# Sample key steps moved out of the prompt's attention into the projections, with GpSimd taking three of four of the first 80 key products

## What is computed

```python
def _project(x, pos, norm1_w, w_in, q_norm_w, k_norm_w):
    h = _rmsnorm(x, norm1_w)
    p = h @ w_in
    ...
    q = _rope(_rmsnorm(q, q_norm_w), pos)
    k = _rope(_rmsnorm(k, k_norm_w), pos)
    return q, k, v, u

def _scores(q, k):
    s = jnp.einsum('bqhcd,bkhcd->bhcqk', q, k, preferred_element_type=jnp.float32)
    return s * (QK_DIM ** -0.5)

def _diff_attn_sample(q, k_new, v_new, k_past, v_past, lam):
    s = jnp.concatenate([_scores(q, k_past), jnp.where(causal, _scores(q, k_new), NEG)], axis=-1)
    a = _diff_weights(s, lam)
    o_past = jnp.einsum('bhqk,bkhd->bqhd', a[..., :n_past], v_past.astype(jnp.float32))
    ...
```

## Time and profile before

| | us |
|---|---|
| median of 3 runs | 1733.65 (1730.45 to 1736.07) |
| the profiled execution | 1735.41 |
| its span in the trace | 1733.7 |
| TensorE busy | 1474.0 (85%) |
| VectorE busy | 782.4 (45%) |
| ScalarE busy | 356.0 (21%) |
| GpSimd busy | 96.7 (6%) |
| DMA, mean over the span | 345 GB/s, 598.10 MB |

### The profile page before, as it was taken

The page is one execution under the profiler, slowest core; times in us unless marked ns, Lnnn a source line. Parts: engine busy times, 40 slices in busy tenths (PEclk is TensorE's granted clock), DMA queues, the critical chain, the costliest instruction groups (busy, mean ns, idle before and its releaser), DMA issues.

```text
span 1733.7 us, 32093 instructions
## 1 busy us (share of the span) xinstructions
PE 1474.0 (85%) x11950; PEld 595.0 (34%) x11951; DVE 782.4 (45%) x1160; ACT 356.0 (21%) x822; POOL 96.7 (6%) x173
## 2 busy tenths in 40 slices
PE   3868887779788978899998998999899999899970
PEld 2433333346433354332332332333233332232320
DVE  2789879997786335221332232132132131131326
ACT  3212212222222111111211211212112122121220
POOL 0000010000000000000100000000000000000000
PEclk8989995679898857999999999999899999999995
DMA  9557888988998785598999999999999999999986
GB/s 327 182 187 258 283 295 272 331 279 292 311 301 270 242 352 207 227 392 339 429 420 403 427 417 396 412 418 411 392 421 412 401 428 411 397 428 399 428 351 253
DMA packets 127292, 598.10 MB, mean 345 GB/s; under 512 B 20503, under 2 KB 20517, under 8 KB 102026
## 3 DMA queue, kind: packets, MB, share of 16 engines
q1 hardware_dynamic: 109088, 560.20, 81.9%
q10 hardware_dynamic: 8634, 20.00, 3.4%
q0 software_dynamic: 9504, 17.06, 2.6%
HBM read 589.36 MB, written 25.87 MB: 355 GB/s over the span
## 4 chain that ended last, share of the span: by engine, by line
PE 40%; DMA 19%; DVE 2%; issue 1%; ACT 0%; DVEq 0%; SPq 0%; ACTq 0%
PE bank L1511 25%; DMA wts<-in_w_gate_up 16%; PE bank L1548 8%; PE bank L1530 4%; DMA wts<-in_w_down 3%; PE bank L1501 1%; PE bank L1618 1%; DVE v_ring L2139 1%; PE bank L1559 1%; PE bank L1599 0%; DVE q_b L2139 0%; DMA h_tok<-h_rows,v_tok 0%; ACT k_T L1155 0%; DVEq L2127 0%; ACT k_T L1138 0%
## 5 line engine op out<-in xcount | busy, mean ns | idle before, releaser
L1511 PE MATMUL bank<-wts,h_T 128*32 128x512 f32 x4032 | 443.9, 597 | 9.7 <-DMA wts<-in_w_gate_up 5.2
L2061 DVE TENSOR_SCALAR q_T<-bank 128x512 f32<-128x512 f32 x32 | 22.1, 692 | 636.9 <-PE bank L1511 636.9
L1511 PEld LDWEIGHTS bank<-wts,h_T 128*32 128x32 f32 x4032 | 129.5, 111 | 308.3 <-issue 296.4
L1548 PE MATMUL bank<-wts,k_T 128*32 128x512 f32 x2048 | 228.3, 597 | 8.0 <-issue 4.9
L1530 PE MATMUL bank<-wts,h_T 128*32 128x512 f32 x992 | 132.6, 675 | 52.2 <-DMA wts<-in_w_gate_up 50.4
L1658 DVE TENSOR_TENSOR wts<-wts,q_b 128x1024 f32<-128x1024 f32 x128 | 158.1, 1235 | 23.1 <-DMA wts<-in_cache_k 17.4
L1661 DVE TENSOR_REDUCE sc<-wts 128x16 f32<-128x1024 f32 x128 | 156.2, 1220 | 4.4
L1145 ACT ACTIVATE h_T<-bank 128x512 f32<-128x512 f32 x66 | 35.9, 595 | 573.5 <-PE bank L1501 573.5
L1548 PEld LDWEIGHTS bank<-wts,k_T 128*32 128x32 f32 x2048 | 64.9, 110 | 149.0 <-issue 139.5
L1223 PE MATMUL bank<-wts,h_T 128*8 128x128 f32 (+1 forms) x480 | 92.7, 465 | 12.3 <-ACT h_T L854 6.4
L1155 ACT ACTIVATE k_T<-bank 32x256 f32<-32x256 f32 x256 | 95.7, 374 | 13.6 <-PE bank L1548 10.2
(11 more groups left out here) (330 smaller groups left out, 1375.8 us busy)
## 6 DMA issues: line engine op xcount, KB each, us to landing
wts<-in_w_gate_up SPq DMA_DIRECT2D x126, 2048.0 KB, 15.8
wts<-in_w_down SPq DMA_DIRECT2D x64, 2048.0 KB, 18.3
wts<-in_cache_k SPq DMA_DIRECT2D x256, 256.0 KB, 3.7
v_ring<-in_cache_v SPq DMA_DIRECT2D x160, 256.0 KB, 3.8
wts<-in_cache_v SPq DMA_DIRECT2D x96, 256.0 KB, 3.9
wts<-in_w_in SPq DMA_DIRECT2D x5, 2048.0 KB, 24.1
wts<-y_rows SPq DMA_DIRECT2D x4, 2048.0 KB, 15.1
wts<-in_w_out ACTq DMA_DIRECT2D x8, 512.0 KB, 6.2
```

Source lines behind the costliest of these rows:

```text
L1511: m = nc.tensor.matmul(PS[part][p0:p0 + 32, :], lhs[:, 32 * b:32 * b + 32], rhs[:, part * F + half * 512:part * F + half * 512 + 512], sta ...
L1548: m = nc.tensor.matmul(PS[4][p0:p0 + 32, :], act_T[0][:, k, a0:a0 + 32], chunk[c][:, k, n * 512:(n + 1) * 512], start=(c == 0 and k == 0), ...
```

## The change

Three things are changed together.

1. The weights in `SCHEDULE`. In the projections of tiles 2 to 4 each stage now brings 1.45 key steps where it brought 1. In the attention each unit brings 0.2 where it brought 1.4 in two places, and the norm's place 0 where it brought 1. The values' weights stay as they are. The number of key steps in the table's other parts stays too.
2. Of the first 80 groups, those whose number modulo 4 is 0, 1 or 2 have their product on GpSimd, as two pieces of 128x512 (`PIECE = 512`) that signal `kprod_done`. VectorE waits for these counts and does the reduction alone. Group 3 of each four, and all from 80 on, stay with VectorE as before. GpSimd now walks through the same table; its tap products come at units 4 to 7 of the attention in that table, behind all of its key products, and its index tables in part L.
3. The semaphores `xw_loaded` and `y_loaded` become one, `rows_in`.

```diff
+        KEYS = 1.45
         for s in range(1, TILES + 1):
             if s > 1:
-                plan(("P", s), 1, both=s > 2)
-            plan(("P", s - 1), 1 if s > 1 else 0, both=s > 2)
-            plan(("P", s), 1 if s > 1 else 3, both=s > 2)
+                plan(("P", s), KEYS, values=1 if s > 2 else 0)
+            plan(("P", s - 1), KEYS if s > 1 else 0, values=1 if s > 2 else 0)
...
-            plan(("P", s), 1)
-            plan(("P", s), 1, 1, 1, both=True)
+            plan(("P", s), KEYS)
+            plan(("P", s), *[KEYS] * 3, values=1)
             if s < TILES:
-                plan(("P", s + 1), 1, both=True)
-            plan(("P", s), 2, values=1)
-            plan(("P", s), 1, 1, both=True)
+                plan(("P", s + 1), KEYS, values=1)
+            plan(("P", s), 2 * KEYS, values=1)
+            plan(("P", s), *[KEYS] * 2, values=1)
             if s < TILES:
-                plan(("P", s + 1), 1, both=True)
-        plan(("P", TILES), 1, 1, both=True)
+                plan(("P", s + 1), KEYS, values=1)
...
-                plan(("Q", j), 1, both=True)
+                plan(("Q", j), 0.2, values=1)
...
-                plan(("Q", j), 0.4, values=0.7)
+                plan(("Q", j), 0, values=0.7)
...
-                plan(("N", (j - 1) // H), 1, both=True)
+                plan(("N", (j - 1) // H), 0, values=1)
...
+        PIECE = 512
+        KEYS_ON_POOL, KEYS_SHARED = (3, 4), 80
+
+        def on_pool(n):
+
+            return n < KEYS_SHARED and n % KEYS_ON_POOL[1] < KEYS_ON_POOL[0]
+
+        def first_on_pool(b):
+
+            return next((g for g in range(NG) if on_pool(b * NG + g)), None)
+
+        def products_on_pool(n):
+
+            return sum(on_pool(m) for m in range(n + 1)) * GP * (AW // PIECE)
...
+            def key_step(b, g):
+                r, n = g % RING, b * NG + g
+                if not on_pool(n):
+                    return
+                if first_on_pool(b) == g:
+                    pool.wait_ge(qb_in, 32 if b == 0 else 16 * (b + 1))
+                pool.wait_ge(k_full[r], 16 * GP * (4 * b + g // RING + 1))
+                for p in range(GP):
+                    for c0 in range(0, AW, PIECE):
+                        cols = slice(c0, c0 + PIECE)
+                        nc.gpsimd.tensor_tensor(k_ring[:, r, p, cols], k_ring[:, r, p, cols],
+                                                q_b[:, b % 2, cols], ALU.mult).then_inc(kprod_done, 1)
+
+            def value_step(b, g):
+                pass
+
+            run_with_samples(key_step, value_step, {part: part_q(part[1]) if part[0] == "Q" else
+                                                    part_l(part[1]) if part[0] == "L" else iter(())
+                                                    for part in a_no})
...
-                dve.wait_ge(k_full[r], 16 * GP * (4 * b + g // RING + 1))
-                V.link(mul(k_ring[:, r, :, :], k_ring[:, r, :, :],
-                           q_b[:, b % 2, :].unsqueeze(1).to_broadcast([P, GP, AW])))
+                if on_pool(b * NG + g):
+                    dve.wait_ge(kprod_done, products_on_pool(b * NG + g))
+                else:
+                    dve.wait_ge(k_full[r], 16 * GP * (4 * b + g // RING + 1))
+                    V.link(mul(k_ring[:, r, :, :], k_ring[:, r, :, :],
+                               q_b[:, b % 2, :].unsqueeze(1).to_broadcast([P, GP, AW])))
```

More of the change, by code:

```diff
@@ L341, in hybrid_step @@
         v_full = [sem(f"v_full{n}") for n in range(VRING)]
-        xw_loaded = [sem(f"xw_loaded{n}") for n in range(TILES + 1)]
+        rows_in = [sem(f"rows_in{n}") for n in range(TILES + 1)]
         win_in = [sem(f"win_in{n}") for n in range(5)]
@@ L683, in _ @@
                       allow_small_or_imprecise_dtypes=True).then_inc(pool_consts, 1)
[L686 to L693, removed]
-                                        w_T[:, ct, :].unsqueeze(2).to_broadcast([P, TAPS + 1, 32]), ALU.mult
-                                        ).then_inc(taps_done, 1)
@@ new lines, in part_l @@
+            def part_l(g):
+                if g == 0:
+                    pool.wait_ge(o_full, UNITS)
+                    pool.wait_ge(v_out, 16 * TILES)
+                    V.link(pool.iota(iota_e[:, :], [[1, E]], base=0, channel_multiplier=0,
+                                     allow_small_or_imprecise_dtypes=True))
+                    V.link(pool.affine_select(out=upper, in_=ones[:, :], compare_op=ALU.is_gt, fill=0.0,
+                                              base=0, pattern=[[1, P]], channel_multiplier=-1))
+                    V.link(pool.iota(row_key, [[-1, E]], base=E - 1, channel_multiplier=0,
+                                     allow_small_or_imprecise_dtypes=True))
+                    V.link(nc.gpsimd.memset(row_key[:, 0:1], -2 * FIRST_KEY))
+                    V.link(nc.gpsimd.memset(row_key[:, 1:2], -FIRST_KEY))
+                    V.link(pool.iota(col_key, [[0, 1]], base=E - 1, channel_multiplier=-1,
+                                     allow_small_or_imprecise_dtypes=True))
+                    V.link(nc.gpsimd.memset(col_key[0:1, :], -2 * FIRST_KEY))
+                    V.link(pool.affine_select(out=col_key, in_=col_key, compare_op=ALU.not_equal, fill=-FIRST_KEY,
+                                              base=-1, pattern=[[0, 1]], channel_multiplier=1))
+                    yield
+                    V.link(pool.iota(col_e, [[0, 1]], base=0, channel_multiplier=1,
+                                     allow_small_or_imprecise_dtypes=True))
+                    V.link(pool.iota(col_tab, [[1, TCOLS]], base=0, channel_multiplier=0))
+                    V.link(pool.iota(pair_no, [[TOPK * P, TILES + 1], [1, TOPK]], base=1, channel_multiplier=TOPK,
+                                     allow_small_or_imprecise_dtypes=True))
+                    pool.iota(iota_r, [[1, CAP]], base=0, channel_multiplier=0,
+                              allow_small_or_imprecise_dtypes=True).then_inc(ids_done, 1)
+                yield
@@ L1821, in part_w @@
                     if c == 0:
-                        dve.wait_ge(xw_loaded[u], 16)
+                        dve.wait_ge(rows_in[u], 16)
                     if s:
@@ L2136, in _ @@
                 m, acc = rows_of(TAIL[u]), out_acc[u]
-                dve.wait_ge(y_loaded[u], 16)
+                dve.wait_ge(rows_in[u], 32)
                 for k in range(TOPK):
```

48 lines of the change are left out of this document (21 added, 27 removed).

## The result

The change makes the kernel slower. The median went from 1733.35 us (four runs beside it) to **1763.45 us** (four runs, 1760.84 to 1765.70): a ratio of 1.017, 95% interval 1.015 to 1.020. The forecast was 1706 us in a range of 1682 to 1738, so even the range missed it. The span in the trace is 1762.3 us.

What follows compares the result with a forecast made beforehand. VectorE was taken to bound tile 1 and the attention, with VectorE, TensorE and transfers nearly level in tiles 2 to 4. Terms -11 + 8 - 28 + 3 = -28 us gave 1706 us, range 1682 to 1738.

Steps and rivals of the forecast that it cites:

- What is moved: Key groups done at each place: 22 for 20, 77 for 58, 85 for 87; 75 us of VectorE products go to GpSimd.
- A product on GpSimd: Cost of a key group's product on GpSimd, read from tap products: 2.0 us, ends 1.9 and 2.9.
- 55 to 117 us: Projections of tile 1, sample keys alone: key ring at 2.0 us a group against 2.39, -11 us, ends -3 and -11.
- 117 to 264 us: Tiles 2 to 4, keys and values: transfers bind at 145 us, times 1.07 gives 155, +8 us, ends -2 and +26.
- rival D: Key ring becomes the slower bound in tiles 2 to 4: 3.5 us a group, +45 there, 1743 us total; chance 0.12.
- 264 to 388 us: Prompt attention: 96 us, the middle between chain and TensorE, so -28 us, ends -42 and -16.
- The chain of 82 us: Prompt attention's lower end: VectorE's other work, keys, ScalarE's exps and tap products one after another, 82 us.
- the end by TensorE: Prompt attention's other end: TensorE busy 94 us at clock 0.67, half of 30 idle us remaining, 108 us.
- 388 us on: Convolution and tail, 388 to 658 us: two key groups more, +3 us, ends 0 and +5.
- the work that was costed at nothing: kprod_done counts in place of k_full, merged semaphores and the two halves of GpSimd's tables: no cost.
- B: All streams: transfers at their limit in tiles 2 to 4, TensorE at 2.4 GHz in attention; -52, 1682 us; chance 0.17.
- C: Gain handed back: tiles 2 to 4 keep ratio 1.19 (+26), attention stays with TensorE at 0.67 (-16); 1736 us; chance 0.16.

## Why the prediction was wrong

The sign was wrong, and three of the four terms missed their ends on the same side. The sum was -11 + 8 - 28 + 3 = -28; measured were +4.5, +39.2, -11.5 (from pmax of sample 2 to the tap, 1.6 - 13.2) and -1.6, in all +30.5.

**What is moved** held, and so did the bytes, 47.9 MB by the forecast. All queues of the changed kernel, 122 to 308 us:

```profile
DMA packets 26085, 48.10 MB, mean 259 GB/s; under 512 B 2897, under 2 KB 2897, under 8 KB 26076
```

**A product on GpSimd** was mis-sized: 2.54 us a group by the median, 2.82 by the mean, for 2.0. It lay inside the ends (1.9 and 2.9), and the choice fell to the wrong one, by a row with broadcast inputs. The estimate by the Trainium skill (GPSIMD Engine Reference, Performance versus the Vector engine), 2.25, was nearer and still too low. Half products, 1.09 us less a group, gave 9.7 us in tiles 2 to 4 and 4.4 in tile 1; the 0.54 us that were missed are worth about half of that, an estimate from that run. So the size alone doesn't explain the loss.

**55 to 117 us**, -11 forecast, +4.5 measured, outside both ends. The step that failed is "while it is at that, the ring fills up and is caught up on later", and with it the pace of 2.0 us a group. Timeline after, GpSimd, VectorE and SyncE's queue:

```profile
82.81 9.55 POOL L755 TENSOR_TENSOR wts<-wts,q_b 128x512 f32<-128x512 f32 x5
82.89 2.26 DVE L1703 TENSOR_TENSOR qk<-qk,stp 128x1024 f32<-128x1024 f32 x1
84.17 15.76 SPq L521 DMA_DIRECT2D wts<-in_cache_k  x7
85.19 2.17 DVE L1703 TENSOR_TENSOR rot<-qk,cw 128x1024 f32<-128x1024 f32 x1
87.39 2.17 DVE L1703 TENSOR_TENSOR qk<-qk,cw 128x1024 f32<-128x1024 f32 x1
89.60 3.31 DVE L1700 TENSOR_TENSOR rot<-rot,qk 128x512 f32<-128x512 f32 x2
92.94 1.22 DVE L1706 TENSOR_REDUCE sc<-wts 128x16 f32<-128x1024 f32 x1
...
98.57 2.50 POOL L755 TENSOR_TENSOR wts<-wts,q_b 128x512 f32<-128x512 f32 x2 [6.21 <-DMA wts<-in_cache_k]
```

The rotary work of a tile keeps VectorE from its reductions for 10 us, longer than alone because its two-input products take 2.2 us beside GpSimd's instead of 1.2. Four slots hold four groups: GpSimd gets that far, and then starves for 6.2 us, since a slot is freed by the reduction. So VectorE's other work counts in full and more, not as 6 of 9. Nor is anything caught up on later. Later reductions on VectorE, with nothing but key steps between them:

```profile
101.10 1.22 DVE L1706 TENSOR_REDUCE sc<-wts 128x16 f32<-128x1024 f32 x1 [1.58 <-POOL wts L755]
...
120.21 1.22 DVE L1706 TENSOR_REDUCE sc<-wts 128x16 f32<-128x1024 f32 x1 [1.22 <-POOL wts L755]
```

These lie eight groups apart, 2.39 us each, the pace of before and not 2.0; over 22 groups that alone is 8.6 of the 15.5 us that the term was off. The forecast's own lap with 2.54 us for the product gives 2.15, so the rest of the pace stays open. All this is read from rows and not isolated by a run; that a shorter product takes back 4.4 us fits.

**117 to 264 us**, +8 forecast, +39 measured, above the upper end of +26. The step that failed is the form of the sum: the largest of four bounds, times 1.07 because "one bound stands well above the others". The transfers weren't that bound (DMA share 0.78, 0.60 with half the key bytes at -9 us). What the runs show in its place is that keys come too late for the denser table. Shortening the way of a key at any of three places gave time back: 13.6 us by SyncE's order, 9.7 by the product, 8.7 by the landing, and 26.1 by the first two. For this stretch the forecast had issue and product only as totals of their engines, and no time to landing at all. The stretch takes 185.6/55 = 3.37 us a group, 13.5 for four. Before it was 146.4/38 = 3.85, so a group did not get slower: 17 more were asked for, and they did not fit into the time of before. That these times are the sum of one slot's lap is argued, not measured.

This is nearest to **rival D**, which had 0.12. It priced 192 us for the stretch, measured were 185.6. That is in part luck: D got there by 0.7 us for GpSimd's product and 0.5 for the lock in each lap, and with all products on VectorE, where neither is, the stretch is as long, 183.9 us, near VectorE's own limit. What D did not have is that SyncE's order alone is worth a third of what was lost in this stretch, and by the medians 20 of the 30 us of the whole kernel. The argument against it, that the DMA bound "already holds that price", was wrong, since the time that a load takes to arrive and the rate of transfers are not the same price.

**264 to 388 us**, -28 forecast, -11.5 measured, beyond the end of -16. Two terms were wrong. (The four tap products, which have 2 us in it, ran ahead of the first score, from 310.9 us.) The chain of 82 us had for waiting only ScalarE's exps, 19.7 us. VectorE is idle for 41 of the 103 us, and the largest wait is of that size:

```profile
L1812 DVE RECIPROCAL stq<-stq 128x2 f32<-128x2 f32 x16 | 2.6, 164 | 22.5 <-ACT qk L1014 22.5
```

What the sum left out is the rest: 7.1 us for TensorE's scores, 5.6 for ScalarE's copy of an attention tile ahead of its norm, 3.0 for keys, and some 3 in small gaps. And the end by TensorE (108 us; half of 30 idle us on top of 94 is 109) was read as TensorE's total work with half its idle time, which the run with fewer value products contradicts: less work, same time, lower clock. 103 us plus 9.7 ahead of it come near 108 for another reason. The chain is what is left over after the totals are excluded; its parts weren't isolated one by one, which stays open. That fewer long VectorE steps shorten the attention was right in kind: 20 key steps (48 us of VectorE) taken out gave 13 us.

**388 us on**, +3 forecast, -1.6 measured, just below the end of 0 and of no weight. Of the work that was costed at nothing (the merged semaphores, GpSimd's tables in halves) no row shows a price.

**The rivals.** B fell with the transfers. C put the loss at the right place but capped it at the ratio of before, 1.19; 185.6 is 1.28 times 145. Its cause ("a late product of GpSimd holds VectorE, and with it the rotary work that TensorE waits for") is seen in the trace, 66 us of waiting for GpSimd, but isn't needed for the loss, since the table without GpSimd is as slow. D would have given the sum had it been joined with C's attention and a first stretch at zero: 0 + 45 - 16 + 3 = +32, as is easy to say afterwards. Every case kept the first stretch at -11, and none joined D's +45 with C's -16, but all three terms went the same way. That is why the range missed.

Of the signs named ahead, those for "wrong" came: pieces just over 1.4 us in the mean (1.41, with a median of 1.27); in tiles 2 to 4 a DMA share of 0.78 with VectorE waiting for GpSimd, which was D's sign; and TensorE's wait for the first pmax 13.9 us long instead of nearly gone. The attention from first score to first tap took 103 us at 0.70, past the 100 of the forecast and short of C's 105 at 0.67.

## What to carry to other kernels

Before believing a bound by totals of the engines, follow one load around a ring of few slots: product, reduction, the issuing queue's place behind other loads, issue, landing. Divide by the slots and compare. Here that came out within a few us for the product and at twice the effect for the landing, so it is a warning and not a formula. Asking for more per unit of time from such a ring can cost even when no engine is full, and moving one of its operations to an idle engine gave nothing here, where that engine takes twice as long for it. An edit that is to test a limit has to change the wait that sets the limit: moving a load in its queue left the ring as deep as it was. When several terms of a sum are unsure in the same direction, one case has to hold them all.

## What the runs showed of the hardware

GpSimd's product of two full SBUF inputs, 128x512, takes 1.27 us, 128x256 0.727 us: 2.1 ns an element and 0.18 us. Its tap products of before with broadcast inputs took 1.908 us for 1024, 1.9 ns an element with all in: at 1024 the full ones would take 2.35 us by that line, an estimate from those two sizes, so the broadcast ones are cheaper by a fifth of that. A memset of 128x512 takes 0.52 us.

Beside GpSimd's products not only VectorE's large products wait. With the products in the attention a TENSOR_SCALAR of 128x2 took 0.49 us in the mean for 0.17, a TENSOR_TENSOR of 128x1 0.47 for 0.16, and single ones up to 0.96 and 1.14. The Trainium skill (SBUF — State Buffer, Who interferes with whom) has an exclusive lock for a VectorE instruction with two SBUF inputs against a GpSimd one that reads SBUF, "not with one that only writes it", and for a tensor_scalar in a 2-port mode. The trace agrees with the first: in the run with memsets the four TENSOR_TENSORs beside memsets alone took 0.16 us, like the nine beside nothing, and the three longer ones (0.53, 0.51 and 1.62 us) overlapped a tap product, which reads. The SCALAR_TENSOR_TENSOR stayed at 0.551 us in the mean. The rotary products, 2.2 us for 1.22 beside GpSimd's, fit it too. It agrees with the second in kind: the TENSOR_SCALAR of 128x2 took 0.3 to 0.6 us in seven of the ten cases beside memsets alone, for 0.17. In which mode it ran no run here shows.

What I had not expected is the price: the waits on instructions as short as that, in a chain, added up to 17.6 us, where 19 products taken off their engine gave 23.
